# DeltaNet levels: query rows and Pool's products moved behind the first levels, both level products in one PSUM bank, router matrix stationary

## The reference, cut to what matters

```python
# gated delta rule, for a chunk of tokens, each head and direction
decay = where(causal, exp(gc_i - gc_j), 0)
A = where(strict, (k*beta) @ k.T * decay, 0)
tmat = inverse(eye + A)                    # lower triangular
u = tmat @ (v * beta);  w = tmat @ (k * beta * exp(gc))
qk = q @ k.T * decay
v_new = u - w @ s
o = (q * exp(gc)) @ s + qk @ v_new
s = s * exp(g_last) + (k * exp(g_last - gc)).T @ v_new
# router, once in each layer
scores = sigmoid(h @ router_w.T)           # 384 tokens x 16 experts
```

## Time and profile before

| | |
|---|---|
| median of 3 runs | 2019.43 us (2017.17 to 2020.03) |
| the profiled execution's own time | 2022.41 us |
| its span, first to last instruction | 2020.4 us |
| mean granted TensorE clock, as a share of 2.4 GHz | 0.874 |
| busy share of the span | PE 86%, PEld 54%, DVE 28%, ACT 23%, POOL 8% |
| the six steps | 242 to 456 us and 645 to 866 us of the span |
| the two routers | from 981 and from 1653 us |

### The profile page before, as it was taken

How to read it: one execution, slowest core, us unless ns; L and a number is a source line. 1 busy time by engine, 2 the same in 40 slices (tenths; PEclk the granted TensorE clock), 3 DMA queues, 4 the chain that set the end, 5 groups by cost and what they waited for, 6 DMA issues and landing times.

```text
span 2020.4 us, 21014 instructions
## 1 busy us (share of the span) xinstructions
PE 1737.1 (86%) x7860; PEld 1099.6 (54%) x7860; DVE 569.1 (28%) x1293; ACT 454.8 (23%) x833; POOL 159.6 (8%) x188
## 2 busy tenths in 40 slices
PE   5799998897999989879599999669888877999984
PEld 3455677794556879755454333247666555433333
DVE  1564324523744343310400000045233232000002
ACT  2154412211544211110111111124333111111111
POOL 0010012200101021100000000102222001000001
PEclk8899867978998866789699999978999878999997
DMA  8122124131212244310559999640030254799982
GB/s 356 42 85 82 64 104 158 52 126 54 94 63 77 91 187 136 125 42 21 245 221 366 403 407 406 240 163 6 6 135 10 115 229 161 314 403 404 398 332 100
DMA packets 65335, 354.79 MB, mean 176 GB/s; under 512 B 7952, under 2 KB 8208, under 8 KB 28240
## 3 DMA queue, kind: packets, MB, share of 16 engines
q1 hardware_dynamic: 47888, 316.69, 39.8%
q10 hardware_dynamic: 13888, 24.13, 3.5%
q0 software_dynamic: 3456, 12.58, 1.7%
HBM read 331.87 MB, written 27.27 MB: 178 GB/s over the span
## 4 chain that ended last, share of the span: by engine, by line
PE 70%; DVE 11%; DMA 8%; ACT 5%; issue 4%; SPq 1%; ACTq 0%; DVEq 0%; POOL 0%; POOLq 0%
PE bank L660 10%; PE bank L881 7%; PE bank L899 4%; PE bank L761 4%; PE bank L932 4%; PE bank L820 4%; PE bank L745 4%; DMA work<-ws 4%; DMA ring<-ws 3%; PE bank L1086 3%; PE bank L944 2%; PE bank L1152 2%; PE bank L769 2%; PE bank L593 2%; PE bank L608 2%
## 5 line engine op out<-in xcount | busy, mean ns | idle before, releaser
L660 PE MATMUL bank<-hT,ring 128*128 128x384 f32 x768 | 265.9, 505 | 15.1 <-issue 10.4
L660 PEld LDWEIGHTS bank<-hT,ring 128*128 128x128 f32 x768 | 149.6, 198 | 122.9 <-issue 23.5
L1086 PE MATMUL bank<-hT,ring 128*128 128x384 f32 x256 | 92.7, 527 | 15.1 <-ACT work L1486 13.5
L881 PE MATMUL bank<-ring,work 128*128 128x512 f32 x192 | 90.5, 625 | 10.6 <-DMA ring<-ws 10.5
L1992 DVE TENSOR_TENSOR work<-bank,work 128x512 f32<-128x512 f32 x12 | 8.3, 694 | 305.7 <-PE bank L881 305.7
L761 PEld LDWEIGHTS bank<-work 128*128 128x128 f32 x576 | 88.2, 242 | 10.6 <-issue 10.6
L761 PE MATMUL bank<-work 128*128 128x64 f32 x576 | 92.9, 329 | 0.0
L820 PE MATMUL bank<-mix,ring 128*128 128x384 f32 x256 | 85.1, 496 | 8.7 <-DVE mix L1862 8.7
L881 PE MATMUL bank<-work 128*128 128x512 f32 x192 | 87.0, 605 | 6.3 <-DMA work<-ws 6.2
L587 PE MATMUL bank<-ring,small 128*32 128x256 f32 x768 | 75.2, 531 | 20.0 <-DMA ring<-ws 20.0
L1313 ACT ACTIVATE work<-bank 128x512 f32<-128x512 f32 x72 | 42.1, 597 | 218.8 <-PE bank L769 180.5
(11 more groups left out here) (349 smaller groups left out, 2565.0 us busy)
## 6 DMA issues: line engine op xcount, KB each, us to landing
ring<-ws SPq DMA_DIRECT2D x192, 1024.0 KB, 9.0
work<-ws SPq DMA_DIRECT2D x96, 1024.0 KB, 14.0
y_slots<-work ACTq DMA_DIRECT2D x24, 256.0 KB, 7.0
x_slots<-s_gla SPq DMA_DIRECT2D x22, 256.0 KB, 6.6
work<-x_slots ACTq DMA_DIRECT2D x40, 128.0 KB, 6.8
y_slots<-work ACTq DMA_DIRECT2D x40, 128.0 KB, 7.5
work<-x_slots ACTq DMA_DIRECT2D x16, 256.0 KB, 7.7
work<-lruw_in ACTq DMA_DIRECT2D x8, 256.0 KB, 2.9
```

The lines of the kernel that those rows point to most:

```text
L660: last = mm(bank[b % 2][:, 0:T], w[:, b % 2, k, :], hT[:, k, :], start=(k == 0), stop=(k == KD - 1))
L881: last = mm(bank[2 + kind][:], xg[p % 2][:, k, :], w[:, k % 4, :], start=(k == 0), stop=(k == KD - 1))
L1086: last = mm(bank[2 * i + m][:, 0:T], w[:, m, k, :], hT[:, k, :], start=(k == 0), stop=(k == KD - 1))
```

## The change

- **Key rows first.** L725's place keeps only the `rowA` products, VectorE's arguments there only `N`, ScalarE's exponentials only that of `N`.
- **Query rows in the levels.** The `rowQ` products of direction 0 come behind the transposes of level 1, those of direction 1 behind level 2, into `bk[2]`. VectorE adds the column and the mask to them behind level 2 (direction 0) and level 3 (direction 1), and ScalarE takes the exponentials of `QK` and `qe` there.
- **Pool** waits at the start of a step until both first `U` are made, and for its last two products until the later exponentials are there.
- **One bank.** L761's product goes to the second half of `bk[1]` instead of `bk[2]`.
- **Router.** Two 16-column blocks of the router matrix are the stationary operand (32 columns), h the moving one with 384 columns. Eight products go to four groups of 32 partitions of bank 6, ScalarE copies the result to `logits`, and three products with a constant `fold16`, which adds the right blocks, give the same 128 x 16 tiles in bank 7. They stand behind the transposes of the first token tile.

```diff
 _C: + ("fold16", 16)
+    put("fold16", (j % 32 == np.arange(16)[None, :] + 16 * (j // 32 % 2)).astype(np.float32))
+        logits = tk(T)
 # TensorE, front of a step
-                        for n, row in enumerate((rowA, rowQ)):
-                            for h in range(H):
-                                last = mm(bk[n][:, h * P:(h + 1) * P],
-                                          pick_row(4 * x + h),
-                                          row[:, c * P:(c + 1) * P], start=True, stop=True)
+                        for h in range(H):
+                            last = mm(bk[0][:, h * P:(h + 1) * P], pick_row(4 * x + h), rowA[:, c * P:(c + 1) * P],
+                                      start=True, stop=True)
                         last.then_inc(bc_done, 1)
 # TensorE, levels
-                                last = mm(bk[2][:, h * 64:(h + 1) * 64], q["Tm"][:, h, :], q["Ys"][:, h, :],
+                                last = mm(bk[1][:, 256 + h * 64:320 + h * 64], q["Tm"][:, h, :], q["Ys"][:, h, :],
 ...
+                        if 1 <= lv < 3:
+                            x, c, q, bk = both[lv - 1]
+                            for h in range(H):
+                                last = mm(bk[2][:, h * P:(h + 1) * P], pick_row(4 * x + h), rowQ[:, c * P:(c + 1) * P],
+                                          start=True, stop=True)
+                            last.then_inc(bc_done, 1)
 # TensorE, router
-                for t in range(NT):
-                    for k in range(KD):
-                        last = mm(bank[7][:, t * E:(t + 1) * E], hT[:, k, t * P:(t + 1) * P], rw[:, k, :],
-                                  start=(k == 0), stop=(k == KD - 1))
+                for k in range(KD):
+                    j, pair = 32 * (k % 4), rw[:, k - k % 2:k - k % 2 + 2, :].rearrange("p a e -> p (a e)")
+                    last = mm(bank[6][j:j + 32, 0:T], pair, hT[:, k, :], start=(k < 4), stop=(k >= 4))
                 last.then_inc(router_done, 1)
 ...
+                        if t == 0 and half == 1:
+                            pe.wait_ge(logits_read, layer + 1)
+                            for u in range(NT):
+                                rows = mm(bank[7][:, u * E:(u + 1) * E], logits[:, u * P:(u + 1) * P], cc("fold16"),
+                                          start=True, stop=True)
+                            rows.then_inc(router_done, 1)
 # ScalarE, front, levels, router
-                        A(q["N"], q["N"], ACT.Exp)
-                        A(q["QK"], q["QK"], ACT.Exp)
-                        A(q["qe"].rearrange("p a b -> p (a b)"), bk[1][:], ACT.Exp).then_inc(exp_done, 1)
+                        A(q["N"], q["N"], ACT.Exp).then_inc(exp_done, 1)
 ...
+                        if 2 <= lv < 4:
+                            x = lv - 2
+                            q, bk = quad[x], bank[3 * x:3 * x + 3]
+                            act.wait_ge(arg_done, g * 12 + (2 * q0 + 2 + x + 1))
+                            A(q["QK"], q["QK"], ACT.Exp)
+                            A(q["qe"].rearrange("p a b -> p (a b)"), bk[2][:], ACT.Exp).then_inc(exp_done, 1)
 ...
+                A(logits, bank[6][:, 0:T], ACT.Copy).then_inc(logits_read, 1)
 # Pool
+                        pool.wait_ge(u_done, g * 42 + (q0 * 7 + 2))
                         TT(q["kdec"], kTok[:, c], bc3(ecols[:, 3, c, 4 * x:4 * x + 4], P), ALU.mult)
                         TT(q["vb"], vTok[:, c], bc3(ecols[:, 1, c, 4 * x:4 * x + 4], P), ALU.mult)
-                        pool.wait_ge(exp_done, g * 6 + (q0 + x + 1))
+                        pool.wait_ge(exp_done, g * 12 + (2 * q0 + 2 + x + 1))
                         TT(q["QK"], q["QK"], Qs[:, c], ALU.mult)
 # VectorE, front and levels
-                            STT(q["N"][:, h, :], bk[0][:, h * P:(h + 1) * P], nc_,
-                                cc("neg_strict", x * P, x * P + P), ALU.add, ALU.add)
-                            last = STT(q["QK"][:, h, :], bk[1][:, h * P:(h + 1) * P], nc_,
-                                       cc("neg_incl", x * P, x * P + P), ALU.add, ALU.add)
+                            last = STT(q["N"][:, h, :], bk[0][:, h * P:(h + 1) * P], nc_,
+                                       cc("neg_strict", x * P, x * P + P), ALU.add, ALU.add)
 ...
-                            TT(uv, uv, bk[2][:, 0:256].rearrange("p (h q b) -> p h q b", h=H, b=b), ALU.subtract)\
+                            TT(uv, uv, bk[1][:, 256:512].rearrange("p (h q b) -> p h q b", h=H, b=b), ALU.subtract)\
                                 .then_inc(u_done, 1)
+                        if 2 <= lv < 4:
+                            x, c, q, bk = both[lv - 2]
+                            dve.wait_ge(bc_done, g * 12 + (2 * q0 + 2 + x + 1))
+                            for h in range(H):
+                                last = STT(q["QK"][:, h, :], bk[2][:, h * P:(h + 1) * P],
+                                           cols[:, 0, c, 4 * x + h:4 * x + h + 1],
+                                           cc("neg_incl", x * P, x * P + P), ALU.add, ALU.add)
+                            last.then_inc(arg_done, 1)
```

More of the change, by code:

```diff
@@ L65 @@
 _C = [("ident", 128), ("ones", 1), ("neg_strict", 256), ("neg_incl", 256), ("pair", 256),
-      ("lev", 768), ("fold", 2), ("ehead", 32), ("sgn", 1), ("bwd", 1), ("eps", 1), ("neg1", 1), ("i16", 16),
+      ("lev", 768), ("fold", 2), ("fold16", 16), ("ehead", 32), ("sgn", 1), ("bwd", 1), ("eps", 1), ("neg1", 1), ("i16", 16),
       ("i4", 4), ("first", 16), ("place", 16)]
@@ L411, in build @@
         router_sig = sem("router_sig")
+        logits_read = sem("logits_read")
         gate_done = sem("gate_done")
@@ L1295, in _ @@
                         q, bk = quad[x], bank[3 * x:3 * x + 3]
-                        act.wait_ge(arg_done, g * 6 + (q0 + x + 1))
-                        A(q["N"], q["N"], ACT.Exp)
-                        A(q["QK"], q["QK"], ACT.Exp)
-                        A(q["qe"].rearrange("p a b -> p (a b)"), bk[1][:], ACT.Exp).then_inc(exp_done, 1)
+                        act.wait_ge(arg_done, g * 12 + (2 * q0 + x + 1))
+                        A(q["N"], q["N"], ACT.Exp).then_inc(exp_done, 1)
                     n = (STEP0[stp] + 3) % RING
@@ L1327, in experts @@
             def experts(layer):
-                act.wait_ge(router_done, 3 * layer + 1)
+                act.wait_ge(router_done, 4 * layer + 1)
+                A(logits, bank[6][:, 0:T], ACT.Copy).then_inc(logits_read, 1)
+                act.wait_ge(router_done, 4 * layer + 2)
                 A(rt_s.rearrange("p a b -> p (a b)"), bank[7][:, 0:NT * E], ACT.Sigmoid).then_inc(router_sig, 1)
-                act.wait_ge(router_done, 3 * layer + 2)
+                act.wait_ge(router_done, 4 * layer + 3)
                 for t in range(NT):
@@ L1785, in _ @@
                     for x, c, q, bk in both:
-                        dve.wait_ge(bc_done, g * 6 + (q0 + x + 1))
+                        dve.wait_ge(bc_done, g * 12 + (2 * q0 + x + 1))
                         for h in range(H):
                             nc_ = cols[:, 0, c, 4 * x + h:4 * x + h + 1]
-                            STT(q["N"][:, h, :], bk[0][:, h * P:(h + 1) * P], nc_,
-                                cc("neg_strict", x * P, x * P + P), ALU.add, ALU.add)
-                            last = STT(q["QK"][:, h, :], bk[1][:, h * P:(h + 1) * P], nc_,
-                                       cc("neg_incl", x * P, x * P + P), ALU.add, ALU.add)
+                            last = STT(q["N"][:, h, :], bk[0][:, h * P:(h + 1) * P], nc_,
+                                       cc("neg_strict", x * P, x * P + P), ALU.add, ALU.add)
                         last.then_inc(arg_done, 1)
                     for x, c, q, bk in both:
-                        dve.wait_ge(exp_done, g * 6 + (q0 + x + 1))
+                        dve.wait_ge(exp_done, g * 12 + (2 * q0 + x + 1))
                         TT(q["N"], q["N"], Gs[:, c], ALU.mult).then_inc(n_done, 1)
@@ L1916, in route @@
                 L(TT(gates_, rt_a, bc3(rt_k, E), ALU.mult))
-                dve.wait_ge(router_done, 3 * layer + 3)
+                dve.wait_ge(router_done, 4 * layer + 4)
                 L(TT(rank[:, :, 0:E], bank[7][:, 64:64 + NT * E].rearrange("p (t e) -> p t e", t=NT), rt_m, ALU.mult))
```

## The result

The kernel after takes 1944.8 us (median of four runs, 1941.0 to 1947.2), the kernel before beside it 2018.3 us: a ratio of 0.964 (95% interval 0.961 to 0.968). That is 73.5 us less, where 35.6 us were forecast.

What follows compares the result with a forecast made beforehand. TensorE, carrying 70% of the chain of waits, bounds the kernel through its waits and lower clock. Terms -41.4 - 6 + 15.6 - 7.8 + 4 = -35.6 us gave 1984 us; own range 1965 to 1996, over the cases 1950 to 2012.

Steps and rivals of the forecast that it cites:

- The front: Start of each DeltaNet step, up to turning the modulation rows: turn starts 7.0 or 6.7 us earlier, -41.4 us in all.
- Turning and U transposes: Behind the front: partly at the higher clock, gain 0 to 2.5 us a step, taken as 1.0, 6 us in all.
- The query rows: Eight-row products moved behind levels 1 and 2: twelve at 0.96 to 1.67 us, taken as 1.3, 15.6 us lost.
- Pool 0: Pool's delayed products beside VectorE's in the levels: contention priced at 0, other bound 20 us.
- shared bank 0: Both level products in one bank: product and correction follow each other in a chain as before, priced at 0.
- The router: In front of each expert stage: sigmoid 3.9 us earlier in each of two layers, -7.8 us, bounds 0 and 13 us.
- The clock in the levels: Levels of the steps: 160 us at 1.2 GHz as before, plus one slow level for the query rows, +4 us.
- this sign: Total 1.2 GHz time in the steps far from 160 us, named as what would make the time wrong most.
- Its argument against: Against the clock mostly holding (1947 us, chance 0.18): turning, copies and transposes still lie in a row.
- six more levels at 5.0 us: Upper end of the rival that low stretches grow without eating the gain: two to six levels, 1994 to 2012 us, chance 0.17.
- The line theory: From the experiments: the gain beyond forecast comes from the front's lines themselves being worth more than reckoned, not from the clock.
- "slower" rival: Query rows between levels keep or bring the clock down, some fourteen more slow levels: 2050 us, chance 0.09.

Runs made afterwards that it cites:

- e10: Kernel before with Pool's wait for U, the router part and the shared bank, query rows left in the front: 1918.1 us.
- e1: Kernel before with the change's router part alone: 2007.2 us, ratio 0.988.
- e6: Kernel after with nine more VectorE products ahead of the second direction's U in each step, putting TensorE's idle gap back: 2059.8 us.
- e9: e6 with ten unused TensorE products in each step, eight in the gap ahead of the turning of the modulation rows, two behind it: 1988.1 us.
- e12: Kernel before with nine unused TensorE products: six in the front's gap, one ahead of the turn, two behind it: 1972.3 us, ratio 0.982.
- e2: Kernel before with only Pool's wait until U is made added: 1927.4 us, ratio 0.958.
- e7: Kernel after with three unused TensorE products in each step, one ahead of the turn and two behind it: 1934.1 us.
- e8: Kernel after with two unused TensorE products (1.3 us) ahead of the key rows in each group's second step: 1953.3 us.
- e13: e10 with two unused TensorE products (1.3 us) ahead of each group's second step: 1916.5 us.
- e3: Kernel after without Pool's wait for U: 1949.0 us.
- e5: Kernel before with Pool's wait for U and the router part together: 1916.0 us, ratio 0.947.
- e11: Kernel after with the query row products also issued in the front, into a bank nobody reads: 1962.8 us.
- e14: Kernel after with four unused TensorE products (2.6 us) ahead of each group's second step: 1947.1 us.
- e15: Kernel after with three unused TensorE products around the turn in the second steps alone: 1942.6 us.

## Why the prediction was wrong

*The front, -41.4 us: right in sum.* To the turn the sum went from 95.8 to 53.4 us, 42.4 us won. TensorE and ScalarE's copies come last there in four steps, as said. In the two second steps they do not: VectorE's L1817 releases the turn, 0.84 us after TensorE was done, and these are the two steps that fall. The share of each edit was not asked and is other than it looks: Pool's wait alone gives 21 us of it.

*Turning and U transposes, -6 us:* 13.0 us, near the upper bound of 2.5 us a step, because the clock holds there in all six.

*The query rows, +15.6 us: right in sum.* The group of L775 in the view by lines:

```profile
L775 PE MATMUL bank<-work,cst 8*128 8x128 f32 x96 | 14.8, 295 | 0.0
```

Eleven of the twelve take 1.15 us, one 2.07 us: each is dearer than priced (0.96 and 1.67 us), and nearly all ran at the higher clock, so two misses met. *Pool 0, shared bank 0: right* (masks stay at 0.42 us beside Pool; e10). *The router, -7.8 us: right in sum;* the sigmoid comes 4.6 and 5.7 us earlier, more than the 3.9 us forecast for each layer, but of these 10.3 us only 7.9 us show in e1's span and 7.4 us in the stretch from the first router to the end.

*The clock in the levels, +4 us: this is the step that failed.* The prediction left the low time "as before"; in the rests it was 159 us and became 89 us. (Its 160 us are another sum, six stretches that begin near the turn; that the two agree is chance.) It had named this sign itself as the one that would make the time most wrong. At the prediction's own price, 1 - 5.86/10.84 = 0.46 us for each low us, that is 70 x 0.46 = 32 us won instead of 4 lost. With it the rest closes: 314.6 + 14.8 - 32 = 297 us, measured 297.3. All terms together: -42.4 - 13.0 + 14.8 - 32 - 7.4 = -80 us; the profiled spans differ by 75.7 us, since the first step begins 3.0 us later and the stretches between the steps and the router are 1.4 us longer.

That the closed gap is the cause is shown: putting it back costs 115 us where its delay accounts for 34 (e6), filling it and the turn with work gives 72 us back at the same delay (e9), filling the front and turn of before wins 46 us in the medians and 37 us by the ratio with nothing else changed (e12), and closing it with one line, turn and levels untouched, takes low time in the rests from 159 to 14 us (e2). The Trainium skill's "HAM oscillation — how this bites in real kernels" (TensorE: Matmul & The Clock Gate) says of waits between bursts of products that TensorE falls to the low clock in them, and stays up when the bursts follow on. These four runs agree with it, by the figures above, and the prediction gave it too little weight. Its argument against, that turning, copies and transposes still lie in a row, holds for all six steps of the kernel after, and four of them stay at 2.4 GHz: the row alone does not bring the clock down.

Three smaller slips of the prediction change nothing here: six more levels at 5.0 us give 2014 us and not 2012, the forecast's own range with turning at 0 ends at 2002 us and not 1996, and the rise at 352.2 says nothing for or against transposes as work, since half a unit (at 349.39) and a level's products had run just before.

*The line theory falls.* For every kernel of the table the rest, less 14.8 us where the query rows are in the levels and less 0.46 us for each low us, is 240 to 245 us: before 241.5, after 241.5, e2 244.4, e6 243.3, e12 241.5. The levels' work, query rows apart, never changed; the clock did.

*What the query rows' move is worth* neither the prediction nor its rivals asked. After against e10: 21.3 us won to the turn, 14.8 us lost in the levels, and 75 us more at 1.2 GHz, 35 us; in the steps' sums the move costs 26 us, and 27 us in time. So the "slower" rival was wrong for the whole change but right about this part's sign. Its mechanism was half right. The first fall of the second steps comes at the turn, ahead of any query row, and steps that enter their levels at 2.4 GHz hold through the query rows (e7, and four steps of the kernel after). But in a step that has fallen, the clock comes back and falls again behind query rows: e8 and e13 have the same delay and a first fall at the same place (13.6 and 10.2 us long in e8, 13.7 us twice in e13), and with the query rows in the levels 24.8 and 23.9 us are low in the rest, without them 11. In the kernel after, group 1's second step falls again at 696.5 and 706.7 us, each 2 us behind query rows, 13.7 of its 30.7 us.

*What goes with a fall.* Take the steps whose gap is closed and whose turn is not filled: all six of after, e2, e3, e5, e8, e10, e11, e13 and e14, and the first and third ones of e15, 58 in all. In 14 of them the turn still waits about 0.8 us for VectorE; 12 of these have over 10 us low in the rest. In 44 it waits 0.2 us for ScalarE (two: 0.4 us for VectorE); only two of these do, both in e11. So a small wait for VectorE that is left ahead of the turn goes with the fall, and in e15 both moved on to the third steps together. With the query rows in the front, as in e10, TensorE's units and ScalarE's copies end after VectorE, and the wait is 0.19 us in all six steps. That the wait is the cause is not shown: no run took it away alone.

*Left open:* the exceptions. e11's second steps fall with a wait of 0.19 us, a third step of e14 holds with 0.79 us, and the two second steps of e14, with 0.87 us each, differ by 36 us. A rule that always says beforehand which step falls did not come out. Nor is it shown that e10's order holds in every place; one delay of its second steps (e13), in both groups, is all there is.

## What to carry to other kernels

Where a gap of TensorE sits ahead of a long run of small products, price the run at both clocks and let the gap decide the forecast, not "as before": here the gap's length was worth 34 us and the clock behind it 70 us and more. Look which engine releases TensorE ahead of such a run, in every step and not in one: here the two steps that fell were the two where it was VectorE. Split a change before crediting it: one wait on Pool alone won more than the whole change, and the move that looked like its core cost 26 us. Where thin work can't be avoided, unused dense products beside it can pay for themselves (e7), but a fill in one step may merely hand the fall to the next (e15).

## What the runs showed of the hardware that was not expected

The price of the low clock was constant over seventeen profiles: 0.46 us for each us at 1.2 GHz, to within 3 us on rests of 250 to 370 us. A 1.2 GHz stretch that begins ahead of the turn can last through four of the six levels; one window of e6, its second step, columns as above:

```profile
328.00:382.70 54.70, 51.10 (x251) 0.50 0.34 136
```

TensorE is busy for 51.1 of these 54.7 us, and four levels do not bring the clock back, while the levels of e2's six steps, entered at 2.4 GHz, have 14 us low in all. And Pool's 128x512 products beside VectorE's (1.59 instead of 0.69 us for one) were worth 88 us (e2), 21 us of it in the fronts and most of the others through the clock, though Pool is busy for only 8% of the span of the kernel before.
